# A two-layer transformer step with halved feed-forward products: another order of the work of ACT, DVE and the load queue

## The reference

```python
    x = x + rmsnorm(mix, nm_post)
    hf = jnp.einsum('btd,df->btf', rmsnorm(x, nf_pre), w_up)
    f = jnp.einsum('btf,fd->btd', jnp.square(jax.nn.relu(hf)), w_down)
    x = x + rmsnorm(f, nf_post)
```

## Time and profile before

| what | value |
|---|---|
| median of 3 runs | 2626.05 us (2624.3 to 2627.3) |
| the profiled execution's own time | 2623.43 us |
| its span in the profile | 2621.5 us |
| PE busy | 2476.4 us, 94% of the span |
| DVE, POOL, ACT busy | 1564.5, 1028.0, 981.8 us |
| mean granted clock of PE | 0.983 |

### The profile page before, as it was taken

How to read it: one execution, slowest core, us unless ns; L and a number is a source line. 1 busy time by engine, 2 the same in 40 slices (tenths; PEclk the granted TensorE clock), 3 DMA queues, 4 the chain that set the end, 5 groups by cost and what they waited for, 6 DMA issues and landing times.

```text
span 2621.5 us, 47149 instructions
## 1 busy us (share of the span) xinstructions
PE 2476.4 (94%) x18500; PEld 2220.4 (85%) x18500; DVE 1564.5 (60%) x2018; ACT 981.8 (37%) x1489; POOL 1028.0 (39%) x435
## 2 busy tenths in 40 slices
PE   8999999998799999999999999999977999999998
PEld 6995666987799999999989866669777999999997
DVE  5456666268566546654765566652786575457546
ACT  3125655144323323333441255542433233323334
POOL 2431000306665566564223300003166655665541
PEclk9999999999999999999999999999989999999999
DMA  6114322324645633563431243222337445434533
GB/s 225 43 39 130 89 82 74 115 83 147 247 152 202 221 139 128 199 221 124 139 115 44 60 119 88 83 68 108 107 141 257 150 177 214 171 131 172 213 134 147
DMA packets 192523, 360.39 MB, mean 137 GB/s; under 512 B 34160, under 2 KB 46640, under 8 KB 192368
## 3 DMA queue, kind: packets, MB, share of 16 engines
q1 hardware_dynamic: 122080, 211.44, 24.3%
q10 hardware_dynamic: 67728, 138.42, 14.4%
q0 software_dynamic: 2560, 8.39, 1.1%
HBM read 305.91 MB, written 49.06 MB: 135 GB/s over the span
## 4 chain that ended last, share of the span: by engine, by line
PE 64%; issue 9%; DVE 8%; POOLq 6%; ACT 4%; DMA 4%; POOL 2%; DVEq 1%; ACTq 1%; SPq 1%
PE psum L2870 18%; PE psum L2913 12%; PE psum L2378 11%; PE psum L2568 3%; PE psum L2363 3%; PE psum L2594 3%; DMA h_quarters<-hl 2%; PE psum L2580 2%; PE psum L2471 2%; PE psum L2615 2%; POOLq L821 2%; POOLq L814 2%; POOLq L818 1%; PE psum L2408 1%; POOL wl L798 1%
## 5 line engine op out<-in xcount | busy, mean ns | idle before, releaser
L2913 PE MATMUL psum<-hidh,wh 128*128 128x264 f32 x1344 | 395.4, 294 | 69.5 <-POOL wl L798 30.7
L2870 PE MATMUL psum<-hh,wh 128*128 128x264 f32 x1344 | 384.9, 286 | 24.6 <-POOL wl L798 23.6
L2913 PE MATMUL psum<-hidl,wh 128*128 128x264 f32 x1344 | 391.1, 291 | 0.0
L2913 PE MATMUL psum<-hidh,wl 128*128 128x264 f32 x1344 | 390.2, 290 | 0.0
L2870 PE MATMUL psum<-hh,wl 128*128 128x264 f32 x1344 | 383.6, 285 | 0.0
L2870 PE MATMUL psum<-hl,wh 128*128 128x264 f32 x1344 | 383.4, 285 | 0.0
L2097 DVE TENSOR_TENSOR z<-psum,z 128x528 f32<-128x528 f32 x360 | 245.9, 703 | 155.1 <-PE psum L2913 154.8
L2913 PEld LDWEIGHTS psum<-hidh,wh 128*128 128x128 f32 x1344 | 261.9, 195 | 77.5 <-issue 56.9
L2870 PEld LDWEIGHTS psum<-hh,wh 128*128 128x128 f32 x1344 | 255.4, 190 | 25.7 <-POOL wl L798 24.5
L2913 PEld LDWEIGHTS psum<-hidl,wh 128*128 128x128 f32 x1344 | 262.2, 195 | 0.0
L2913 PEld LDWEIGHTS psum<-hidh,wl 128*128 128x128 f32 x1344 | 262.0, 195 | 0.0
(11 more groups left out here) (318 smaller groups left out, 5863.5 us busy)
## 6 DMA issues: line engine op xcount, KB each, us to landing
hh<-h_quarters ACTq DMA_DIRECT2D x62, 1056.0 KB, 5.9
hl<-h_quarters ACTq DMA_DIRECT2D x62, 1056.0 KB, 8.5
raw<-wst SPq DMA_DIRECT2D x48, 512.0 KB, 3.6
z<-cache_c SPq DMA_DIRECT2D x352, 64.0 KB
x<-x_spill SPq DMA_DIRECT2D x4, 4224.0 KB, 14.4
sacc<-wst SPq DMA_DIRECT2D x56, 256.0 KB, 3.3
t<-wst SPq DMA_DIRECT2D x56, 256.0 KB, 3.0
cn<-wst SPq DMA_DIRECT2D x56, 256.0 KB, 4.1
```

The lines of the kernel that those rows point to most:

```text
L2870: ins = pe.matmul(psum[:, up_bank(st, u) + q, 0:HW], w[:, o:o + P], m[:, 4 * kh + k, nh * HB + q * HW:nh * HB + q * HW + HW], start=(fresh ...
L2913: ins = pe.matmul(psum[:, 2 * u + q, 0:HW], w[:, o:o + P], m[:, t, k * HB + q * HW:k * HB + q * HW + HW], start=(fresh and k == 0 and n == ...
```

## The change

The change moves instructions within the streams of SP, ACT and DVE. Nothing is added, removed or resized.

- SP, before block 0: the quarters a11 and a12 of the first down weights are loaded ahead of a21 and a22; the store of `B_22` is issued ahead of the loads of the two up quarters.
- SP, after block 0: the loads of a22 and a21 for block 1 are issued ahead of the store of `T_2`.
- ACT, block 0: weight 3 goes ahead of the high part of the second hidden sum; the last four multiplications by the gain go ahead of the third hidden sum.
- ACT, blocks 1 to 6: weights 8, 9 and 10 each go ahead of one high part of a hidden operand.
- DVE, block 0: the difference for the third hidden sum and `raw_t` go ahead of the low part and of two of the bank reads; the low part of the first difference (`low_t(0)`) goes ahead of `take(5)`.
- DVE, blocks 1 to 6: the low part of b11 goes between the halves of `take(0)`, the next difference goes ahead of the low part of b12, which goes between the halves of `take(1)`.

```diff
 # SP
+                quarter_in(a11, down0, 0, 0, dn_a11)
+                quarter_in(a12, down0, 0, 1, dn_a12)
                 quarter_in(a21, down0, 1, 0, dn_q)
                 quarter_in(a22, down0, 1, 1, dn_q)
-                quarter_in(a11, down0, 0, 0, dn_a11)
-                quarter_in(a12, down0, 0, 1, dn_a12)
+                sp.wait_ge(hl_new.sem, at.whole(hl_new, KD))
+                keep(B_22, 1, hq3_out)
                 splits(0)
                 quarter_in(u22, up1, 1, 1, up_q)
                 splits(1)
                 quarter_in(u21, up1, 1, 0, up_q)
-                sp.wait_ge(hl_new.sem, at.whole(hl_new, KD))
-                keep(B_22, 1, hq3_out)
...
-                sp.wait_ge(t_lo.sem, at.value(t_lo, 2))
-                keep(T_2, 1, hq3_out)
                 at.step(split, N_DN + 1)
                 def weights_of(tile, again, first):
                     quarter_in(a22, tile + 4, 1, 1, dn_q, 0)
                     quarter_in(a21, tile + 4, 1, 0, dn_q)
+                    if first:
+                        sp.wait_ge(t_lo.sem, at.value(t_lo, 2))
+                        keep(T_2, 1, hq3_out)
                     quarter_in(a11, tile + 4, 0, 0, dn_a11, 2)
 # ACT, hidden_parts (block 0)
-                    high_sum(1, both, PH, b11)
                     at.step(s2_new)
                     act.wait_ge(s2_new.sem, at.value(s2_new))
                     high_down(0, 3, a21)
+                    high_sum(1, both, PH, b11)
                     gained(hl_raw, 1, 1, 1, xb_in)
+                    gained(x2, 1, 1, 1, xb_in)
                     high_sum(2, both, 2 * PH, b12)
-                    gained(x2, 1, 1, 1, xb_in)
 # ACT, both_halves (blocks 1 to 6)
                     high_sum(3, both, 0, b12)
-                    high_sum(1, both, PH, b11)
                     new_sum(s2_new)
                     weight(8, a21)
-                    high_sum(2, both, 2 * PH, b12)
+                    high_sum(1, both, PH, b11)
                     new_sum(s3_new)
                     weight(9, a21)
+                    high_sum(2, both, 2 * PH, b12)
+                    weight(10, a22)
                     act.wait_ge(dn_full.sem, at.value(dn_full, 3 * PH))
                     high_hid(0, both, b21)
-                    weight(10, a22)
                     weight(11, a12)
 # DVE, parts_of, blocks 1 to 6
-                        take(0, TURN)
+                        take(0, TURN[:2])
                         low(0, both, b11)
+                        take(0, TURN[2:])
                         dve.drain()
+                        less(b11, b12, b11, both).then_inc(h_sum.sem, 1)
+                        take(1, TURN[:2])
                         low(3, both, b12)
-                        take(1, TURN)
-                        less(b11, b12, b11, both).then_inc(h_sum.sem, 1)
+                        take(1, TURN[2:])
 # DVE, parts_of, block 0
+                    less(b12, b21, b12, two).then_inc(h_sum.sem, 1)
+                    raw_t(2, part_of(hl_raw, 0, 1), part_of(x2, 0, 1), part_of(hl_raw, 0, 1))
                     low(1, both, b11)
-                    less(b12, b21, b12, two).then_inc(h_sum.sem, 1)
-                    take(2, TURN)
-                    raw_t(2, part_of(hl_raw, 0, 1), part_of(x2, 0, 1), part_of(hl_raw, 0, 1))
+                    take(2, TURN[:2])
+                    raw_t(3, part_of(x2, 0, 1), part_of(hl_raw, 1, 1), part_of(x2, 0, 1))
+                    take(2, TURN[2:])
+                    raw_t(3, part_of(hl_raw, 1, 1), part_of(hl_raw, 1, 1), part_of(hl_raw, 0, 1))
                     low(2, both, b12)
-                    take(3, TURN[:2])
-                    raw_t(3, part_of(x2, 0, 1), part_of(hl_raw, 1, 1), part_of(x2, 0, 1))
-                    take(3, TURN[2:])
-                    raw_t(3, part_of(hl_raw, 1, 1), part_of(hl_raw, 1, 1), part_of(hl_raw, 0, 1))
+                    take(3, TURN)
                     low(0, both, b21)
                     take(4, TURN)
-                    take(5, TURN[:2])
                     low_t(0)
-                    take(5, TURN[2:])
+                    take(5, TURN)
```

## The result

| | before | after |
|---|---|---|
| median (runs) | 2626.68 us (4: 2624.3 to 2629.64) | 2582.13 us (4: 2579.91 to 2583.81) |
| ratio after to before, 95% interval | | 0.9829 (0.9812 to 0.9846) |
| the profiled execution's time, its span | 2623.43, 2621.5 us | 2579.91, 2578.1 us |
| mean granted clock of PE | 0.983 | 0.988 |
| PE, DVE, ACT, POOL busy | 2476.4, 1564.5, 981.8, 1028.0 us | 2463.7, 1544.9, 980.2, 1033.2 us |

The change makes the kernel 44.5 us faster, with an interval from 1.5 to 1.9%. The forecast was 2581 us and 45 us. A total that fits can come from terms that are wrong both ways, so I cut both executions into stages, each from its first matmul to the first of the next stage, for both layers.

What follows compares the result with a forecast made beforehand. PE, busy 94% of the span, bounds the kernel, so only its gaps and slower stretches can be won. A 5 + B 4 + C 16 + D 20 = 45 us, giving a median of 2581 us, range 2553 to 2608.

Steps and rivals of the forecast that it cites:

- A: Up stage ahead of block 0: PE's waits for two low parts mostly vanish; 5 us in all, bounds 0 and 6.
- D: Twelve down stages, blocks 1 to 6: weight 8 waits for its slot alone; 20 us, bounds 0 and 50.
- B: Down stage of block 0: ACT saves a wait, `raw_t` moves ahead of bank reads; 4 us, bounds -6 and +15.
- C: Up stage of block 1: POOL's wait for loads goes, product 5 starts sooner; 16 us, bounds 4 and 31.
- its first chain: Up stage of block 1: POOL's 9.15 us wait for a22 and a21, loaded behind `T_2`'s store, goes.
- its second: Up stage of block 1: `T_2`'s store, load back, ACT's copy, weight 4, POOL's low part; product 5 6 us sooner.
- I take 1.7 for all twelve: Down stages of blocks 1 to 6: each gains 1.7 us, 20 us together.
- My replay of POOL and DVE in turns: Down stages, blocks 1 to 6: alternating instructions, product 3 1.9 us sooner, 1.7 back before product 4; net 1.5.
- Rival 1: Down stages, blocks 1 to 6: POOL's chain sets weights 8 and 9, only A, B, C stay; 2601 us, chance 0.17.
- rival 4: Whole kernel: SP's earlier loads were not PE's wait, D 0, C 4, A and B cancel; 2622 us, chance 0.08.
- Rival 2: Down stages, blocks 1 to 6: product 3 waits under 1 us, 26 us more gained; 2555 us, chance 0.15.
- Rival 3: Down stages, blocks 1 to 6: POOL pushed later, 3.3 us wait before product 3, clock falls; 2655 us, chance 0.10.

Runs made afterwards that it cites:

- Kernel 6: Changed kernel with the store of `B_22` again behind the loads of the two up quarters; 2592.11 us, ratio 0.9878.
- kernel 5: Changed kernel with a21 and a22 again loaded ahead of a11 and a12 for block 0; 2583.2 us, ratio 0.9845.
- Kernel 7: Changed kernel with ACT's wait for `T_4`'s store and load of `T_1` moved behind weight 7 and a high part in block 1; 2574.76 us.
- Kernels 2, 3 and 9: Changed kernel with the order in blocks 1 to 6 undone: ACT's (2) 2582.0 us, DVE's (3) 2588.02 us, both (9) 2604.22 us.
- kernel 8: Changed kernel with DVE's last difference in blocks 1 to 6 moved between the halves of `take(2)`; 2575.1 us, ratio 0.9810.
- kernel 12: Kernel 10 with some of DVE's bank reads of products 1 and 2 in block 0 moved earlier; 2565.99 us, ratio 0.9783.
- kernel 1: Changed kernel with the store of `T_2` again ahead of the loads of a22 and a21; 2583.62 us, ratio 0.9843.
- kernel 11: Kernel 10 with the store of `T_2` again ahead of the loads of a22 and a21; 2573.88 us, ratio 0.9805.
- 10: Changed kernel with the edits of kernel 7 and kernel 8 together; 2565.22 us, ratio 0.9775.

## Why the prediction was right, and where not

The total fits better than its terms. A came out 2.3 us larger than forecast and D 4.8 smaller, and 0.7 came from stages that the change does not touch. That the sum is within 1 us of the median's fall is in part luck.

**A: right in its cause, too small, and its cover holds only with the other move.** Both waits vanished. The term was 5 and the stages gave 7.3, above my bound of 6. The estimate of the waits was not at fault: they were 3.3 and 2.3 us in the kernel before, 5.6 together. The rest is that PE's busy time fell too, from 23.98 and 24.11 us to 23.22 in both layers. Against the down stage POOL starts 21.6 - (615.46 - 599.67) = 5.8 us later, where I had counted 3, and "its next products are needed some 7 us after it has made them" leaves out that SP waits for the slots POOL frees. Kernel 6, where the loads of the input stand behind those slots, shows what that can cost; with `B_22`'s store moved ahead of them it is 0.8 us (kernel 5).

**B: right in size, not in its steps.** 4.1 against 4, but 0.6 in layer 0 and 3.5 in layer 1. I had product 3 start 1 us sooner, product 4 1 later and product 5 2 sooner. Measured in layer 0: 0.1 later, 1.8 later, 1.5 sooner. In layer 1, which gave most, product 5 starts only 0.2 us sooner, and the gain comes behind it. The "issue" wait went from 7.56 to 3.29, but a wait of 6.03 appeared inside product 2. The profile puts it to the bank reads of line 2096, which stand behind three differences on DVE that run beside POOL's sums from 626.26 on. Kernel 5, where the first loads are back and POOL is sooner, has 3.1 there. Of `B_22`'s store I counted 2.08 us. In kernel 6 it is worth 7.4 and 7.7, with the first loads ahead of it; the longer wait there is 6.72 us on ACT and 9.31 on PE.

**C: right in size and in its first chain, not in the steps of its second.** 16.1 against 16. POOL's wait for `sacc` is below 2 us, the stages are 49.1 and 48.2 against "near 48". Product 5 starts 7.0 and 8.1 us sooner (I had 6), but the wait of some 5 us before it did not stay; it is 0.30, and 2.11 before product 6. The 6 us were to come as 2 from the store, 1 from the store before it, and 3 from POOL. The first difference's store took 9.2 us where it had taken 7.9. `T_2`'s store was no quicker: issued at 684.51 and 685.08, it landed 10.8 us after the latter, 11.4 in all as before, although the two loads no longer follow it; two loads of the same size on ACT's queue, issued at 680.33 and 680.96, run into it as they did before. What gave time instead was the load back behind it (issues of ACT's queue at 698.29 before and at 695.86 after, us to landing):

```profile
hl_raw<-t_quarters ACTq DMA_DIRECT2D x1, 1056.0 KB, 8.3
hl_raw<-t_quarters ACTq DMA_DIRECT2D x1, 1056.0 KB, 5.2
```

Against the start of the stage the store landed 0.7 us sooner, the load took 3.1 less, and POOL's low part of weight 4 ended 3.2 sooner behind it. That is 7.0 in layer 0. POOL's part was as counted; that the other 3 us came out, from a load and not from the stores, is luck. The Trainium skill (DMA: Bandwidth & Descriptors, section Anatomy of one DMA, for transfers issued from GpSimd) would have had the pair at an estimated 7. `T_2`'s measured 11.4 decides here; the nearest to the estimate is another such pair of the kernel before, issued at 711.12 and landed 7.4 us later.

**D: 15.2 against 20.** The step that failed is "I take 1.7 for all twelve". The ten stages of the loop gave 18.5, or 1.85 each: weight 8's high part comes 0.3 us after product 2's start, product 3 begins 18.6 us into block 3's stage (I had 19.6), waits of 0.8 to 2.6 stand before product 3 and, in nine of the ten, of 1.2 before product 4. But block 1's down stages are not like them. They lost 3.4 us instead of giving 3.4, since with C the stage begins before `T_4`'s store has landed, and ACT waits for it ahead of weight 7. The order of ACT and a store's length in the earlier trace rows were there to be read; I did not ask what an earlier stage would run into. Kernel 7 takes that wait away, and these stages get 3.8 us back, no more, since POOL's loads are next.

D's cause was also too narrow. I wrote "Now weight 8 waits for the slot alone" and put that to ACT's order. Kernels 2, 3 and 9 show that DVE's order does it too: it alone gives the whole, and ACT's alone all but 3.8 of 21 us. My replay of POOL and DVE in turns had the right form, and kernel 8, which makes one instruction of DVE wait instead of POOL's, confirms it. The Trainium skill (SBUF — State Buffer, section SBUF: two separate sides) calls this an exclusive lock for the whole instruction; the trace agrees: POOL's low part went from 3.14 to 2.39 us and DVE's difference from 2.23 to 3.21 with kernel 8.

**The rivals.** Rival 1 (D only changes places) and rival 4 (no change) fall with the ten stages' 18.5. Rival 2 (D gives all) is half met by kernel 8, whose stages of 42.4 are what it had in mind; it takes one more move. Rival 3 (slower, from 3.3 us before product 3 on) did not occur in the loop. It came about in block 1, where PE waited 5.93 and the clock fell to 0.93, for another reason. The range's lower end was said to be rival 2's 2553, where that rival's own sum gives 2555; nothing hangs on it.

**What stays open.** Why block 0's down stage stays at 57.5 to 58 us: kernel 12 excludes the bank reads as the only limit. In it the next wait is for weight 3, behind eight multiplications by the gain, and no kernel here put weight 3 ahead of them or moved POOL's sums. In block 1 the loads that POOL's sum waits for in kernel 7 were not moved. Where the 2.2 us beyond kernel 5's 5.1 in A come from, all of it in layer 0, was not tried either. Nor was it tried why `T_2`'s load back became 3.1 us shorter.

## What to carry to other kernels

When one stage is made to end sooner, list what the next stage's first instructions wait for, and ask which of these ends at a time of its own; here a store did, and it took back 9.1 of 13.4 us (kernel 1), and 2.9 of 11.6 (kernel 11 against 10) once one wait was moved. When a producer is delayed on purpose, follow also the load queue that waits for the slots it frees. Where two streams were reordered together, undo each alone and both: D's two halves are worth 0 and 6 us of the median when undone one at a time, and 22 us together.
